# A two-block model on one core: reordering the activations, the gated scores and the output projection of the even mixer

## The chip, the core and the metric

The kernel runs on one core of a Trainium2 chip. The time is device time in microseconds (us) of that core, from one launch that computes the whole function. A profiled execution gives a span, which is the time between the first and the last thing the profiler records, and, beside it, the execution's own device time, which is a few us longer.

The engines named below are TensorE (PE in the profile; its weight loads are PEld), VectorE (DVE), ScalarE (ACT), GpSimd (POOL) and the queues that start DMAs. Each engine executes its own instructions in order and waits on semaphores that others raise.

## What is computed

The input is 256 tokens of width 1024. A first block (recurrent and attention halves) is followed by a second block of two layers. Layer 0 of the second block has the even mixer, which is what the change touches:

```python
def even_mixer(u, w_in, w_out, lb, onorm_g, sinks, cos_b, sin_b):
    B, S, _ = u.shape
    qa, fa, ia, ga, qb, kb, vb = jnp.split(u @ w_in, EVEN_SPLITS, axis=-1)
    oa = hgrn2_chunkwise(qa.reshape(B, S, A_HEADS, A_DK), fa.reshape(B, S, A_HEADS, A_DK),
                         ia.reshape(B, S, A_HEADS, A_DV), lb.reshape(A_HEADS, A_DK))
    oa = rmsnorm(oa, onorm_g) * jax.nn.silu(ga.reshape(B, S, A_HEADS, A_DV).astype(jnp.float32))
...
    ob = swa_with_sinks(qh, kh, vb.reshape(B, S, B_KV_HEADS, B_HEAD_DIM), sinks).astype(u.dtype)
    return jnp.concatenate([oa, ob], axis=-1) @ w_out
```

with 4 heads of 128 in the gated attention and 8 of 64 in the window attention. Inside the gated attention, for chunks of 64 tokens:

```python
    qf = jax.nn.silu(chunks(q))
    f = lb5 + (1.0 - lb5) * jax.nn.sigmoid(chunks(f_logit))
    k = 1.0 - f
...
    b = jnp.cumsum(jnp.log(f), axis=3)
    b_last = b[:, :, :, -1:, :]
    q_s = qf * jnp.exp(b)
    k_s = k * jnp.exp(-b)
    k_d = k * jnp.exp(b_last - b)
...
    att = jnp.where(causal, jnp.einsum('bhnck,bhnsk->bhncs', q_s, k_s), 0.0)
```

After the mixer come a residual add with a norm, and a feed-forward network (FFN) whose first step needs the normed rows of each token tile.

## The kernel before

Every engine's program is written out by hand in `build`, one block for each engine, and semaphores order them against each other. No scheduler moves anything.

**Weights as units.** All large weights are cut into units of 128 x 2048 floats (1 MB). SyncE loads them into a ring of 4 slots. For each unit ScalarE writes a rounded copy (`whi`, line 420, the helper `hi()`), then VectorE the rest (`wlo = raw - whi`, line 1190, the helper `lo()`), and TensorE multiplies in three passes (lines 2063 to 2065). `hi()` for unit u waits until TensorE has used unit u-4, `lo()` waits for `hi()`, and each engine takes the units in the order in which its program calls the helper. A helper that is called late holds back everything behind it on its engine.

**Token tiles.** The 256 tokens are two tiles of 128, t = 0 and t = 1. `acc[t]` are the PSUM sums. `turn` holds two PSUM buffers for transposes (line 2116), which are used in the order of the list `EVEN_TURNS`, and `aux` two for scores and mixes.

**The even mixer on TensorE.** Its program is a list of 34 slots, 0 to 33; a slot is one unit against one tile, 12 matmuls of 128 x 512 (slot 0 and 4 have some more). Slots 8 to 15 make the forget logits and queries (`fq`), 16 to 23 the values and output gates (`ig`), 24 and 25 a projection for the next layer (`ple1`, unit 12), 26 to 29 the output projection of the window attention (`out_swa`, units 13 and 14, both tiles), 30 to 33 that of the gated attention (`out_hgrn`, units 15 and 16). Small pieces are hooked in ahead of certain slots: the last two window mixes (`swa_mix`, line 2463) at 20 and 22, the last turns of probabilities at 19 and 21, `swa_fed` (transposes of the window output) at 25 and 27, `hgrn_scores` (line 2476, 4 heads) at 26, `hgrn_mix` (lines 2486 and 2489) at 27, `hgrn_fed` at 29 and 31, and `normed_rows` (eight transposes of tile 0 for the FFN) at 33.

**The even mixer on ScalarE.** After the exponentials of the last window head pair (`probs(3)`) stand: Silu of the queries `qsT` (line 905), Sigmoid of the forget logits `fT` (908), `probs_turned(2)` (two copies, 866, for which the mix at slot 20 waits), Ln (912), `values(0)` (844, 846), one `hi()` (unit 12), `probs_turned(3)`, three Exp of 128 x 1024 (`eb`, `ks`, `ebd`, 918 to 921), two `hi()` (units 13 and 14), and `values(1)`. A function of another table set than the last one costs an ACT_TABLE_LOAD ahead of it.

**The even mixer on VectorE.** `kk` from `fT`, `head_out(2)` (the output of window head pair 2), four scans that give b in `fT` (1902), `ebd` (1920), one `lo()` (unit 12), `head_out(3)`, then the scaled queries and keys: `qsT*eb` (1928), `ks` (1929), `kx`, `ky`, `kz` (1932 to 1940). The last of them raises `keys_ready`, for which `hgrn_scores` waits. Then two `lo()` and, per head, the masked copy of the scores `att_a` (1951).

**The tail.** When the last slot of tile 0 is done, ScalarE squares `acc[0]`, GpSimd forms the norm's scale, and VectorE scales, adds to `h` and writes the normed rows `xn` (1253, 1260, 1244), which `normed_rows` transposes.

Of the kernel before, what the change touches and what calls it, by code (L numbers as in the profile page):

```python
# [26 lines left out]
P = 128  # L27
# [87 lines left out]
def build(nc, io):  # L115
    with ExitStack() as ctx:
# [286 lines left out]
        def _(act):  # L403
# [404 lines left out]
            def even():  # L808
# [94 lines left out]
                for name in ("g0", "g1"):  # L903
                    received(name)
                act.activation(qsT[:, :, :], qsT[:, :, :], ACT.Silu).then_inc(q_silu, 1)
# [9 lines left out]
                hi()  # L915
                probs_turned(3)
                act.wait_ge(b_ready, 1)
                act.activation(eb[:, :, :], fT[:, :, :], ACT.Exp).then_inc(ea_ready, 1)
                act.activation(ks[:, :, :], fT[:, :, :], ACT.Exp, scale=-1.0).then_inc(ea_ready, 1)
                act.wait_ge(ebd_in, 1)  # L920
                act.activation(ebd[:, :, :], ebd[:, :, :], ACT.Exp).then_inc(ea_ready, 1)
                hi(2)
# [11 lines left out]
                hi()  # L934
                fed("s1", 4, 1)
                for t in range(TOK):
                    mix()
                    act.activation(xn[:, t, 0:BANK], aux[:, t, :], ACT.Square).then_inc(sq_ready, 1)
                fed("h0", 0, 0)
                hi(2)  # L940
# [3 lines left out]
                square_sum(acc[0][:, :], xn[:, 0, :])  # L944
                feed(feed_hi, 0)
# [223 lines left out]
        def _(dve):  # L1169
# [632 lines left out]
            def even():  # L1802
# [123 lines left out]
                dve.wait_ge(q_silu, 1)  # L1926
                dve.wait_ge(ea_ready, 2)
                mark(dve.tensor_tensor(qsT[:, :, :], qsT[:, :, :], eb[:, :, :], ALU.mult))
# [13 lines left out]
                lo(2)  # L1942
                no_sums(1)
                no_sums(0)
                fed("s0", 4, 0)
                lo()
                no_sums(1, 1)
                for a in range(A_HEADS):
                    n["aux"] += 1
                    dve.wait_ge(aux_ready, n["aux"])  # L1950
                    dve.copy_predicated(att_a[:, a, :], mask_a[:, :].bitcast(I32), aux[:, a % 2, 0:3 * P])\
                        .then_inc(aux_read, 1)
                lo()
                fed("s1", 4, 1)
# [5 lines left out]
                for t in range(TOK):  # L1960
                    dve.wait_ge(rstdm_ready, t + 1)
                    for a in range(A_HEADS):
                        ins = dve.scalar_tensor_tensor(ymix[:, t, P * a:P * a + P], aux[:, t, P * a:P * a + P],
                                                       rsm[:, t, a:a + 1], sga2[:, t, a, :], ALU.mult, ALU.mult)
                        if a < A_HEADS - 1:
                            mark(ins)
                        if a == A_HEADS - 2:
                            settle()
                    ins.then_inc(hgrn_out, 1)
                fed("h0", 0, 0)  # L1970
                lo(2)
# [6 lines left out]
                lo()  # L1978
# [74 lines left out]
        def _(pe):  # L2053
# [350 lines left out]
            def even():  # L2404
# [62 lines left out]
                def hgrn_scores():  # L2467
                    pe.wait_ge(keys_ready, 1)
                    pe.wait_ge(swa_p, B_HEADS // 2)
                    for a in range(A_HEADS):  # L2470
# [45 lines left out]
                slots += [("out_swa", 13 + k, k, t) for t in range(TOK) for k in range(2)]  # L2516
                slots += [("out_hgrn", 15 + k, k, t) for t in range(TOK) for k in range(2)]
                for s, (kind, k, i, t) in enumerate(slots):
# [18 lines left out]
                    if s in SWA_SCORES:  # L2537
                        swa_scores(SWA_SCORES.index(s))
                    if s == 25:
                        swa_fed(0)  # L2540
                    if s == 26:
                        hgrn_scores()
                    if s == 27:
                        swa_fed(1)
                        hgrn_mix()
                    if s in (29, 31):
                        hgrn_fed(0 if s == 29 else 1)
# [238 lines left out]
```

## Time and profile before

| | |
|---|---|
| median of 3 runs | 1446.43 us (1443.91 to 1447.07) |
| profiled execution, device time | 1445.71 us |
| its span | 1442.9 us |
| TensorE busy | 1414.0 us (98%), 6598 matmuls |
| VectorE busy | 871.1 us (60%) |
| ScalarE busy | 711.4 us (49%) |
| GpSimd busy | 79.7 us (6%) |
| DMA | 272.51 MB, mean 189 GB/s |

TensorE's matmuls overlap: a record is longer than the distance to the next start. So its busy share says that it hardly ever stands still, and the useful numbers are the starts in the timeline and the idle time in square brackets, with the engine that ended it. Times within the span count from its start. The even mixer fills the stretch from about 510 to 624 us.

### The profile page before, as it was taken

How to read it: one execution, taken by the hardware profiler on the slowest of the kernel's cores; microseconds unless marked ns; L12 is line 12 of the kernel's file. 1: busy time of each engine (PE TensorE's matmuls, PEld its weight loads, DVE VectorE, ACT ScalarE, POOL GpSimd, SP SyncE). 2: the span in 40 equal slices, each digit the busy share in tenths (PEclk: the TensorE clock that was granted, in tenths of full speed). 3: DMA queues.
4: the chain of work that ended last, by engine and by line, in shares of the span. 5: the costliest groups of instructions: out<-in, count | busy, mean ns of one | idle time of the engine just before them, and what ended most of it. 6: DMA issues, size and time to landing. Idle time of an engine off the chain costs nothing.

```text
span 1442.9 us, 17115 instructions
## 1 busy us (share of the span) xinstructions
PE 1414.0 (98%) x6598; PEld 1169.2 (81%) x6598; DVE 871.1 (60%) x811; ACT 711.4 (49%) x724; POOL 79.7 (6%) x91
## 2 busy tenths in 40 slices
PE   7999999999999999999999999999999999999997
PEld 6788887878888888878888878888888878888886
DVE  6869686776453766764644574644674545654536
ACT  4674765545343457653443553443543445453424
POOL 0000000010000200110000120000202101000001
PEclk9999999999999999999999999999999999999999
DMA  9747554465464553444555464555463533654541
GB/s 393 292 153 262 184 177 158 164 238 212 168 222 156 190 197 117 152 176 182 204 185 186 182 236 173 213 189 184 172 216 134 207 143 124 241 179 170 196 184 44
DMA packets 40380, 272.51 MB, mean 189 GB/s; under 512 B 4609, under 2 KB 5505, under 8 KB 8706
## 3 DMA queue, kind: packets, MB, share of 16 engines
q1 hardware_dynamic: 36864, 261.65, 49.7%
q10 hardware_dynamic: 3458, 10.04, 2.2%
q8 instruction: 42, 0.69, 0.2%
q14 instruction: 16, 0.13, 0.0%
HBM read 270.62 MB, written 1.05 MB: 188 GB/s over the span
## 4 chain that ended last, share of the span: by engine, by line
PE 85%; DVE 7%; ACT 3%; DMA 3%; issue 2%; POOL 0%; SPq 0%; DVEq 0%; POOLq 0%; ACTq 0%
PE acc L2063 26%; PE acc L2065 26%; PE acc L2064 26%; PE turn L2116 3%; DVE wlo L1190 3%; DMA raw<-in_units 2%; ACT whi L420 1%; DMA mod_raw<-in_units 1%; DVE h L1260 1%; DVE xn L1244 1%; PE aux L2600 0%; PE turn L2265 0%; DVE feed_lo L1228 0%; DMA gpost<-in_g_final 0%; DVE xn L1253 0%
## 5 line engine op out<-in xcount | busy, mean ns | idle before, releaser
L1190 DVE TENSOR_TENSOR wlo<-raw,whi 128x2048 fp32r<-128x2048 f32 x233 | 533.0, 2297 | 260.3 <-ACT whi L420 260.2
L2063 PE MATMUL acc<-whi,feed_hi 128*128 128x512 f32 (+1 forms) x1496 | 595.6, 398 | 4.9 <-DVE wlo L1190 4.4
L2065 PE MATMUL acc<-whi,feed_lo 128*128 128x512 f32 (+1 forms) x1496 | 583.1, 390 | 0.0
L2064 PE MATMUL acc<-wlo,feed_hi 128*128 128x512 f32 (+1 forms) x1496 | 582.2, 389 | 0.0
L420 ACT ACTIVATE whi<-raw 128x2048 fp32r<-128x2048 f32 x233 | 445.4, 1916 | 256.1 <-PE acc L2065 241.1
L2063 PEld LDWEIGHTS acc<-whi,feed_hi 128*128 128x128 f32 x1496 | 281.9, 188 | 65.7 <-DVE wlo L1190 6.8
L2065 PEld LDWEIGHTS acc<-whi,feed_lo 128*128 128x128 f32 x1496 | 281.5, 188 | 59.8
L2064 PEld LDWEIGHTS acc<-wlo,feed_hi 128*128 128x128 f32 x1496 | 282.2, 189 | 55.9 <-issue 1.2
L2063 PE MATMUL acc<-whi,hid_hi 128*128 128x512 f32 x352 | 138.0, 392 | 0.0
L2065 PE MATMUL acc<-whi,hid_lo 128*128 128x512 f32 x352 | 137.1, 389 | 0.0
L2064 PE MATMUL acc<-wlo,hid_hi 128*128 128x512 f32 x352 | 137.0, 389 | 0.0
L2065 PEld LDWEIGHTS acc<-whi,hid_lo 128*128 128x128 f32 x352 | 66.1, 188 | 13.8
L2064 PEld LDWEIGHTS acc<-wlo,hid_hi 128*128 128x128 f32 x352 | 66.1, 188 | 13.3
L2063 PEld LDWEIGHTS acc<-whi,hid_hi 128*128 128x128 f32 x352 | 66.1, 188 | 13.3
L679 ACT ACTIVATE hid_hi<-turn 128x512 f32 (+2 forms) x48 | 26.4, 549 | 99.3 <-PE turn L2116 99.3
L1704 DVE TENSOR_TENSOR hid_lo<-turn,hid_hi 128x512 f32 (+2 forms) x48 | 30.8, 642 | 71.8 <-ACT hid_hi L679 71.8
L1090 POOL TENSOR_SCALAR ms<-ss 128x1 f32<-128x1 f32 x18 | 13.6, 756 | 1045.5 <-ACT xn L440 1025.7
L1695 DVE SCALAR_TENSOR_TENSOR hid<-acc,pre_rs,sgl 128x512 f32<-128x512 f32 (+1 forms) x48 | 33.8, 704 | 48.6 <-ACT sgl L672 44.7
L462 ACT ACTIVATE feed_hi<-turn 128x512 fp32r<-128x512 f32 x48 | 26.1, 593 | 55.1 <-PE turn L2116 55.1
L1228 DVE TENSOR_TENSOR feed_lo<-turn,feed_hi 128x512 fp32r<-128x512 f32 x48 | 31.0, 686 | 30.9 <-ACT feed_hi L462 30.8
L672 ACT ACTIVATE sgl<-acc,pre_rs 128x512 f32<-128x512 f32 x40 | 27.2, 680 | 37.6 <-PE acc L2065 37.6
L2116 PE MATMUL turn<-setup,xn 128*128 128x128 f32 x250 | 34.9, 279 | 5.0 <-DVE xn L1244 4.2
(326 smaller groups left out, 860.2 us busy)
## 6 DMA issues: line engine op xcount, KB each, us to landing
raw<-in_units SPq DMA_DIRECT2D x237, 1024.0 KB, 4.9
mod_raw<-in_units SPq DMA_DIRECT2D x6, 1024.0 KB, 10.9
gpost<-in_norm_g ACTq DMA_DIRECT2D x8, 512.0 KB, 4.4
gpre<-in_norm_g ACTq DMA_DIRECT2D x6, 512.0 KB, 5.6
mod_more<-in_units SPq DMA_DIRECT2D x2, 1024.0 KB, 23.4
h<-in_x SPq DMA_DIRECT2D x2, 512.0 KB, 10.3
w_ax<-in_w_ax SPq DMA_DIRECT2D x1, 1024.0 KB, 26.4
bgate<-in_b_gate SPq DMA_DIRECT2D x1, 1024.0 KB, 27.7
```

What stands on the lines that cost most here:

```text
L420: act.activation(whi[:, u % RING, :], raw[:, u % RING, :], ACT.Copy).then_inc(hi_ready, 1)
L462: act.activation(dst[:, 4 * i:4 * i + 4, lanes(t)], turn[:, b, :].rearrange("p (c s) -> p c s", c=4), ACT.Copy).then_inc(fed_hi, 1)
L672: act.activation(sgl[:, t, :, :], acc[t][:, :].rearrange("p (i n) -> p i n", i=2)[:, :, 0:256], ACT.Silu, scale=pre_rs[:, t:t + 1]).then_i ...
L679: act.activation(dst, turn[:, b, 0:P * count].rearrange("p (c s) -> p c s", c=count), ACT.Copy).then_inc(fed_hi, 1)
L1190: dve.tensor_tensor(wlo[:, u % RING, :], raw[:, u % RING, :], whi[:, u % RING, :].bitcast(F32), ALU.subtract).then_inc(lo_ready, 1)
L1228: dve.tensor_tensor(dst[part], turn[:, b, :].rearrange("p (c s) -> p c s", c=4), hi_part[part].bitcast(F32), ALU.subtract).then_inc(moved[ ...
L1695: dve.scalar_tensor_tensor(hid[:, t, 0:tiles, :], up, pre_rs[:, t:t + 1], sgl[:, t, 0:tiles, :], ALU.mult, ALU.mult)\
L1704: dve.tensor_tensor(hid_lo[:, at, lanes(t)], turn[:, b, 0:P * count].rearrange("p (c s) -> p c s", c=count), hid_hi[:, at, lanes(t)].bitca ...
L2063: pe.matmul(out, xh, wh, start=first, stop=False)
L2064: pe.matmul(out, xh, wl, start=False, stop=False)
L2065: return pe.matmul(out, xl, wh, start=False, stop=last)
L2116: last = pe.transpose(turn[:, b, P * i:P * i + P], part, ident[:, :])
```

## The change

Four things are moved; no arithmetic is added or removed.

1. ScalarE: the Silu of the queries goes from ahead of the Sigmoid to behind the three Exps. The Exp of `ks` now comes before that of `eb`. The `hi()` of unit 12 goes from behind `values(0)` to behind the three Exps, ahead of the Silu.
2. VectorE: `qsT*eb` becomes the last step of the keys instead of the first. `keys_ready` is now raised twice, by `kz` and by `qsT*eb`, and the scores wait for the second.
3. TensorE: the scores of heads 0 and 1 are made at slot 24, those of heads 2 and 3 at slot 25 (all four at 26 before). `hgrn_mix` is at 26 (27 before), `hgrn_fed` at 28 and 30 (29 and 31 before). VectorE's masked copies and the `lo()`, `hi()` and feeding steps around them are put in an order that fits.
4. The eight slots of the output projection are interleaved. Slots 26 to 33 were: window tile 0 twice, window tile 1 twice, gated tile 0 twice, gated tile 1 twice. They are now: window tile 0 twice, window tile 1 (unit 13), gated tile 0 twice (units 15 and 16), window tile 1 (unit 14), gated tile 1 twice. Tile 0 is summed at the end of slot 30 instead of 31, so that two slots lie between its sum and `normed_rows` at slot 33 instead of one.

```diff
@@ ScalarE
                 probs(3)
-                for name in ("g0", "g1"):
-                    received(name)
-                act.activation(qsT[:, :, :], qsT[:, :, :], ACT.Silu).then_inc(q_silu, 1)
                 for name in ("f0", "f1"):
                     received(name)
                 act.activation(fT[:, :, :], fT[:, :, :], ACT.Sigmoid).then_inc(f_sig, 1)
...
                 values(0)
-                hi()
                 probs_turned(3)
                 act.wait_ge(b_ready, 1)
+                act.activation(ks[:, :, :], fT[:, :, :], ACT.Exp, scale=-1.0).then_inc(ea_ready, 1)
                 act.activation(eb[:, :, :], fT[:, :, :], ACT.Exp).then_inc(ea_ready, 1)
-                act.activation(ks[:, :, :], fT[:, :, :], ACT.Exp, scale=-1.0).then_inc(ea_ready, 1)
                 act.wait_ge(ebd_in, 1)
                 act.activation(ebd[:, :, :], ebd[:, :, :], ACT.Exp).then_inc(ea_ready, 1)
+                hi()
+                for name in ("g0", "g1"):
+                    received(name)
+                act.activation(qsT[:, :, :], qsT[:, :, :], ACT.Silu).then_inc(q_silu, 1)
                 hi(2)
                 values(1)
...
-                hi()
-                fed("s1", 4, 1)
                 for t in range(TOK):
                     mix()
                     act.activation(xn[:, t, 0:BANK], aux[:, t, :], ACT.Square).then_inc(sq_ready, 1)
+                hi()
+                fed("s1", 4, 1)
                 fed("h0", 0, 0)
-                hi(2)
+                hi()
                 fed("h1", 0, 1)
                 sums(0)
                 square_sum(acc[0][:, :], xn[:, 0, :])
+                hi()
                 feed(feed_hi, 0)
@@ VectorE
                 head_out(3)
-                dve.wait_ge(q_silu, 1)
-                dve.wait_ge(ea_ready, 2)
-                mark(dve.tensor_tensor(qsT[:, :, :], qsT[:, :, :], eb[:, :, :], ALU.mult))
+                dve.wait_ge(ea_ready, 1)
                 mark(dve.tensor_tensor(ks[:, :, :], kk[:, :, :], ks[:, :, :], ALU.mult))
...
                     .then_inc(keys_ready, 1)
-                lo(2)
+                dve.wait_ge(q_silu, 1)
+                dve.tensor_tensor(qsT[:, :, :], qsT[:, :, :], eb[:, :, :], ALU.mult).then_inc(keys_ready, 1)
+                lo()
...
+                attend((0, 1))
                 fed("s0", 4, 0)
+                attend((2, 3))
                 lo()
                 no_sums(1, 1)
-                for a in range(A_HEADS):
...
                 lo()
-                fed("s1", 4, 1)
...
+                fed("s1", 4, 1)
+                lo()
                 fed("h0", 0, 0)
-                lo(2)
+                lo()
                 fed("h1", 0, 1)
...
                 feed(feed_lo, feed_hi, 0)
-                lo()
+                lo(2)
@@ TensorE
-                def hgrn_scores():
-                    pe.wait_ge(keys_ready, 1)
+                def hgrn_scores(heads):
+                    pe.wait_ge(keys_ready, 2)
...
-                slots += [("out_swa", 13 + k, k, t) for t in range(TOK) for k in range(2)]
-                slots += [("out_hgrn", 15 + k, k, t) for t in range(TOK) for k in range(2)]
+                swa, hgrn = ([[(kind, at + k, k, t) for k in range(2)] for t in range(TOK)]
+                             for kind, at in (("out_swa", 13), ("out_hgrn", 15)))
+                slots += swa[0] + swa[1][0:1] + hgrn[0] + swa[1][1:2] + hgrn[1]
...
+                    if s == 24:
+                        hgrn_scores((0, 1))
                     if s == 25:
                         swa_fed(0)
+                        hgrn_scores((2, 3))
                     if s == 26:
-                        hgrn_scores()
+                        hgrn_mix()
                     if s == 27:
                         swa_fed(1)
-                        hgrn_mix()
-                    if s in (29, 31):
-                        hgrn_fed(0 if s == 29 else 1)
+                    if s in (28, 30):
+                        hgrn_fed(0 if s == 28 else 1)
```

How the rows stand on the engines. On ScalarE, from the second half of `values(0)` to the two `hi()` behind the exponentials, before:

```order
L846 ACTIVATE sga_143<-acc,pre_rs 128x512
L420 ACTIVATE whi<-raw 128x2048 [waits unit_used,loaded1]
L866 ACTIVATE pt_147<-turn 128x384 [waits turned0,swa_mixed]
L866 ACTIVATE pt_147<-turn 128x384 [waits turned1]
L918 ACT_TABLE_LOAD
L918 ACTIVATE eb<-fT 128x1024 [waits b_ready]
L919 ACTIVATE ks<-fT 128x1024
L921 ACTIVATE ebd<-ebd 128x1024 [waits ebd_in]
L420 ACTIVATE whi<-raw 128x2048 [waits unit_used,loaded2]
L420 ACTIVATE whi<-raw 128x2048 [waits unit_used,loaded3]
```

and now:

```order
L846 ACTIVATE sga_143<-acc,pre_rs 128x512
L866 ACTIVATE pt_147<-turn 128x384 [waits turned0,swa_mixed]
L866 ACTIVATE pt_147<-turn 128x384 [waits turned1]
L914 ACT_TABLE_LOAD
L914 ACTIVATE ks<-fT 128x1024 [waits b_ready]
L915 ACTIVATE eb<-fT 128x1024
L917 ACTIVATE ebd<-ebd 128x1024 [waits ebd_in]
L420 ACTIVATE whi<-raw 128x2048 [waits unit_used,loaded1]
L921 ACT_TABLE_LOAD
L921 ACTIVATE qsT<-qsT 128x1024 [waits moved1]
L420 ACTIVATE whi<-raw 128x2048 [waits unit_used,loaded2]
L420 ACTIVATE whi<-raw 128x2048 [waits unit_used,loaded3]
```

The rounding of unit 12 (`whi`, loaded1) has moved from ahead of the exponentials to behind them, and the Silu with a table load has come in behind it.

On VectorE, from `ebd` over the `lo()` of unit 12 and `head_out(3)` to the first key, now; the order of these is as before, save that `ks` has taken the place of `qsT*eb` in the last row:

```order
L1921 TENSOR_TENSOR ebd<-fT 128x1024 [waits b_ready]
L1191 TENSOR_TENSOR wlo<-raw,whi 128x2048 [waits hi_ready]
L1849 TENSOR_TENSOR den<-den,esink 128x2x2 [waits sink_exp,swa_p]
L1851 RECIPROCAL rden<-den 128x2x2 [waits dve_step]
L1857 TENSOR_TENSOR ymix<-turn,rden 128x2x64 [waits swa_mixed,dve_step]
L1857 TENSOR_TENSOR ymix<-turn,rden 128x2x64 [waits swa_mixed]
L1928 TENSOR_TENSOR ks<-kk,ks 128x1024 [waits ea_ready]
```

The `wlo` of unit 12 has not moved: it still stands ahead of all keys and waits for the `whi` above.

On TensorE, the beginning of slot 24, before:

```order
L2063 MATMUL acc<-whi,feed_hi 128x512
L2064 MATMUL acc<-wlo,feed_hi 128x512
L2065 MATMUL acc<-whi,feed_lo 128x512
L2063 MATMUL acc<-whi,pT_hi 128x512 [waits lo_ready,ple_lo,acc_free0]
L2064 MATMUL acc<-wlo,pT_hi 128x512
```

and now:

```order
L2070 MATMUL acc<-whi,feed_hi 128x512
L2071 MATMUL acc<-wlo,feed_hi 128x512
L2072 MATMUL acc<-whi,feed_lo 128x512
L2483 MATMUL aux<-qsT,ks 128x64 [waits swa_p,keys_ready,acc_free0]
L2483 MATMUL aux<-qsT,kx 128x64
```

The wait for the keys stood two slots and one set of four transposes later; it now stands ahead of slot 24.

## Rows read from the trace of the kernel before

**Rows 1.** Waits of TensorE, 560 to 640 us: waiting <- waited for: total, times, longest
```profile
PE turn L2116 <- DVE xn L1244: 2.1, 2, 1.4
PE turn L2463 <- ACT pt L866: 1.0, 1, 1.0
PE aux L2476 <- DVE att_a L1951: 0.3, 1, 0.3
```
**Rows 2.** TensorE timeline, slots 19 to 24: start, length, line, operation [idle before]
```profile
566.49 0.39 PE L2065 MATMUL acc<-whi,feed_lo 128*128 128x512 f32 x1
567.87 0.41 PE L2463 MATMUL turn<-vb,pt 128*128 128x64 f32 x2 [0.99 <-ACT pt L866]
...
572.06 0.82 PE L2116 MATMUL turn<-setup,s 128*128 128x128 f32 x6
...
582.31 0.39 PE L2063 MATMUL acc<-whi,pT_hi 128*128 128x512 f32 x1
```
**Rows 3.** TensorE timeline, slots 32 and 33 and the FFN's first units
```profile
616.87 0.39 PE L2064 MATMUL acc<-wlo,feed_hi 128*128 128x512 f32 x1
617.10 0.39 PE L2065 MATMUL acc<-whi,feed_lo 128*128 128x512 f32 x1
...
620.65 0.48 PE L2063 MATMUL acc<-whi,feed_hi 128*128 128x512 f32 x1
...
631.64 1.03 PE L2116 MATMUL turn<-setup,xn 128*128 128x128 f32 x8
632.99 0.50 PE L2063 MATMUL acc<-whi,feed_hi 128*128 128x512 f32 x1 [0.32 <-DVE wlo L1190]
```
**Rows 4.** ScalarE timeline, 562 to 583 us
```profile
562.62 1.28 ACT L905 ACT_TABLE_LOAD   x1
...
565.00 1.28 ACT L908 ACT_TABLE_LOAD   x1
...
567.26 0.85 ACT L866 ACTIVATE pt<-turn 128x384 f32<-128x384 f32 x2
...
572.55 1.90 ACT L420 ACTIVATE whi<-raw 128x2048 fp32r<-128x2048 f32 x1
...
575.21 1.28 ACT L918 ACT_TABLE_LOAD   x1
576.51 1.06 ACT L918 ACTIVATE eb<-fT 128x1024 f32<-128x1024 f32 x1
...
579.37 3.70 ACT L420 ACTIVATE whi<-raw 128x2048 fp32r<-128x2048 f32 x2
```
**Rows 5.** VectorE timeline, from the scans to the end of the keys
```profile
570.05 2.58 DVE L1902 TENSOR_TENSOR_SCAN fT<-reset_a,ff 128x256 f32<-128x256 f32 x4 [0.33 <-ACT ff L912]
...
574.48 2.29 DVE L1190 TENSOR_TENSOR wlo<-raw,whi 128x2048 fp32r<-128x2048 f32 x1 [0.58 <-ACT whi L420]
576.69 0.16 DVE L1848 TENSOR_TENSOR den<-den,esink 128x4 f32<-128x4 f32 x1
...
578.62 1.23 DVE L1928 TENSOR_TENSOR qsT<-qsT,eb 128x1024 f32<-128x1024 f32 x1 [1.03 <-ACT ks L919]
579.76 1.22 DVE L1929 TENSOR_TENSOR ks<-kk,ks 128x1024 f32<-128x1024 f32 x1
...
583.49 4.49 DVE L1190 TENSOR_TENSOR wlo<-raw,whi 128x2048 fp32r<-128x2048 f32 x2
```
**Rows 6.** Stretches: bounds, length, busy of PE, PEld, DVE, ACT, POOL, granted PEclk, DMA
```profile
1435.00:1436.00 1.00, 0.65 (x3) 0.19 (x1) 0.00 (x0) 0.32 (x1) 0.00 (x0) 1.00 0.00 0
1437.00:1438.00 1.00, 0.00 (x0) 0.00 (x0) 0.77 (x2) 0.72 (x2) 0.00 (x0) 0.94 0.00 0
1438.00:1439.00 1.00, 0.00 (x0) 0.00 (x0) 0.00 (x0) 0.00 (x0) 0.81 (x2) 0.50 0.00 0
17.00:18.00 1.00, 0.51 (x3) 0.51 (x3) 1.00 (x2) 0.56 (x2) 0.35 (x1) 1.00 0.99 410
```
**Rows 7.** TensorE timeline, the longest idle time between matmuls near the start
```profile
17.49 1.66 PE L2191 MATMUL aux<-ones,mod_part 128*128 128x1 f32 x7 [2.92 <-DVE mod_part L1312]
```

More of the change, by code:

```diff
@@ L1941, in even, with attend @@
                     .then_inc(keys_ready, 1)
-                lo(2)
+                dve.wait_ge(q_silu, 1)
+                dve.tensor_tensor(qsT[:, :, :], qsT[:, :, :], eb[:, :, :], ALU.mult).then_inc(keys_ready, 1)
+                lo()
+                def attend(heads):
+                    for a in heads:
+                        n["aux"] += 1
+                        dve.wait_ge(aux_ready, n["aux"])
+                        dve.copy_predicated(att_a[:, a, :], mask_a[:, :].bitcast(I32), aux[:, a % 2, 0:3 * P])\
+                            .then_inc(aux_read, 1)
                 no_sums(1)
                 no_sums(0)
+                attend((0, 1))
                 fed("s0", 4, 0)
+                attend((2, 3))
                 lo()
                 no_sums(1, 1)
-                for a in range(A_HEADS):
[L1949 to L1952, printed above, removed]
                 lo()
-                fed("s1", 4, 1)
                 for t in range(TOK):
@@ L2465, in swa_mix @@
                         pe.matmul(out[1], pt2[:, j, 2 * P:], vb[:, 1, kv], start=False, stop=True).then_inc(swa_mixed, 1)
-                def hgrn_scores():
-                    pe.wait_ge(keys_ready, 1)
+                def hgrn_scores(heads):
+                    pe.wait_ge(keys_ready, 2)
                     pe.wait_ge(swa_p, B_HEADS // 2)
-                    for a in range(A_HEADS):
+                    for a in heads:
                         n["aux"] += 1
```

## The prediction

> **What bounds the kernel now.** I read the table of engines first: TensorE is busy nearly all of the span and no other engine is near it, so only what makes TensorE wait, or adds work to it, can move the time. Then the waits of TensorE in the stretch that the change touches: 3.4 us in all, three entries [rows 1]. Then its timeline, to see where each lies, and last the timelines of ScalarE and VectorE there, since a step moved on them costs nothing until TensorE has to wait for it. A matmul record is 0.39 us long, but the next starts 0.23 us after it (616.87 to 617.10 [rows 3]); so a wait costs its recorded idle time plus 0.16 us, or plainly the distance of the starts less 0.23.
>
> **Part 1: the Silu leaves the place ahead of the Sigmoid.** The mix at slot 20 starts 1.38 us after the matmul ahead of it (566.49 to 567.87) where 0.23 is normal, because the two copies `pt` come late [rows 2]. Ahead of the copies stand the Silu and its table load, from 562.62 to 565.00, 2.38 us [rows 4]. Without them the copies run from 564.88 for 0.85 us to 565.73, and TensorE comes at 566.72: the wait goes whole, **-1.15 us**, with 1 us to spare. One table load (1.28 us) goes from ScalarE too, since the queries' Silu and the gates' Silu now follow each other with nothing but copies between; ScalarE is not what ends anything there, so I count nothing for it.
>
> **Part 2: the scores in two halves.** The third head's scores waited 0.3 us for VectorE's masked copy [rows 1]. Between the halves there are now twelve matmuls of slot 24, some 2.7 us, and the wait goes: **-0.46 us**. In exchange TensorE changes once more between small and large matmuls, under 0.1 us, which I leave out.
>
> **Part 3: the interleaved output.** From the last matmul of slot 32 to the first behind the eight transposes are 3.55 us (617.10 to 620.65 [rows 3]), in which both halves of the normed rows are waited for. Eight transposes without that wait take at most 1.03 us (631.64 to 632.99 less the 0.32 that is another wait [rows 3]). So the wait is 3.55 - 0.23 - 1.03 = 2.29 us. The change puts a slot of 2.7 us more between tile 0's sum and these transposes, which is more than the wait: **-2.29 us**. The feeds of the gated output come one slot earlier, but so does the mix, and VectorE's unit steps between are the same in number; I see nothing new that is late. VectorE now has two units instead of one between the tails of tile 0 and tile 1. That is 2.2 us later for tile 1 (one `wlo`, 574.48 to 576.69 [rows 5]), of which most falls into time in which TensorE still multiplies; the wait for the FFN's fourth unit, 0.32 us now [rows 3], grows by 0 to 1.1. I take **+0.2 us**.
>
> **Part 4: the keys must be there at slot 24.** This is the term that the change adds. Slot 24 starts at 582.31 [rows 2], and without part 1's wait at **581.16**. The keys hang on this chain, in the new order:
>
> - the turns at slot 21 start at 572.06 - 1.15 = 570.91 and take 0.82 [rows 2], the second `pt` copy ends some 0.43 later (half of the 0.85 for two [rows 4]): 572.2. The scans are no later: they begin behind `head_out(2)` at about 568.6 and take 2.58 [rows 5], 571.2.
> - table load up to the next ScalarE start, 1.30 (575.21 to 576.51), and three Exps, 2.86 (576.51 to 579.37) [rows 4]: 576.4.
> - the `hi()` of unit 12, which the change puts here, 1.90 [rows 4]: 578.3.
> - the `lo()` of unit 12, which stands on VectorE ahead of all keys and has not moved, so it waits for that `hi()`: 2.21 [rows 5], 580.5. The `hi()` stood at 572.55 before [rows 4], and this `lo()` at 574.48.
> - `head_out(3)`, 0.90 (576.69 to 578.62 less the 1.03 of waiting), then the keys `ks` to `kz`, 3.73 (579.76 to 583.49) [rows 5]: 585.1. ScalarE's Silu is done by then (578.3 + 1.28 + about 1.1 = 580.7), so it is hidden.
> - `qsT*eb`, 1.23 [rows 5]: **586.4**.
>
> TensorE therefore stands still ahead of slot 24 for 586.4 - 581.2 = **+5.2 us**. Behind the waiting matmul are queued slot 24 itself, the window feed and everything after. Before, the same wait lay at slot 26, about 6 us later, and was met with 4.7 us to spare (583.5 against 588.2, two slots and four transposes behind 582.31). The chain's steps are measured ones; what can shift is their places, by 1 us either way.
>
> A ScalarE table switch is priced at about 2.66 us in all, load and drain, by the Trainium skill, "ScalarE: Activation LUTs", section "What ACT_TABLE_LOAD costs". The trace does not agree: the next function starts 1.30 us after the load [rows 4], and the trace decides. By the page's figure the stall would be 6.6 us instead of 5.2.
>
> **The sum without the clock:** -1.15 - 0.46 - 2.29 + 0.2 + 5.2 = **+1.5 us**. Against the profiled execution (1445.71 us, 2.8 above its span) that is 1447.2; against the median of the runs shown, which is 0.7 higher, 1447.9.
>
> **The clock.** A stop of 5.2 us is longer than any between matmuls so far. At the end of the kernel the last matmul ends at 1435.65; the granted clock is 1.00 still in 1436, 0.94 in the stretch 1437 to 1438 and 0.50 after [rows 6]: it fell to the lower level (1.2 GHz of 2.4) 2.2 us after the work ended. Near the start an idle time of 2.92 us passed with the clock at 1.00 [rows 6, 7]. So a fall within 5.2 us is likelier than not. How long TensorE then works at the lower level before it is given 2.4 GHz again, no row shows. I bound it by nothing below and by the length of the stop above, 5.2 us; half of such time is lost, 0 to 2.6 us. I take the middle, **+1.3 us**, which gives +2.8 and **1449.2 us**.
>
> The Trainium skill states the same rule, "TensorE: Matmul & The Clock Gate", section "What's actually happening": the throttled state is the default and activity releases it. It speaks against a change that makes one long stop out of several short ones, also where their sums are equal.
>
> **Rivals.**
>
> - *The clock holds.* For it: it held through 2.92 us. Against it: 5.2 is far longer, and it fell after 2.2 at the end. Then +1.5: 1447.9 us, or down to 1446.9 if the chain is 1 us shorter than I read it.
> - *The clock stays low for long (slower).* The place is slots 24 to 26, behind the stop. From 2.8 us at the lower level on, the loss passes 2.9 us in all; at 5.2 us it is +4.1: 1450.5 us. The scores and slot 24 then take twice their time.
> - *The keys are early (faster).* If the `lo()` of unit 12 did not have to wait for the late `hi()`, VectorE would take it at about 572.4, behind `ebd`, and be through `head_out(3)` at 575.6; the keys would be done at 579.3, and `qsT*eb` would wait for the Silu, 580.7, and end at 581.9. The stop would be 0.8 us, with no fall of the clock, and the sum -1.15 - 0.46 - 2.29 + 0.2 + 0.8 = -2.9: 1443.5 us. Against it: the order of rows shows both helpers where they stand, and `lo()` reads what `hi()` writes. It would take a fault in the reading of units.
> - *The change doesn't do what it says:* the order shows every move as described; I give it nothing.
>
> **How the numbers follow.** What a measurement can tell from no change is about 0.2%, 2.9 us. Forecast (stop, and a clock low for up to 2.8 us): 0.40. Clock holds: 0.23. Clock low for longer: 0.25. Keys early: 0.12. The forecast lies at the edge of 2.9 us, so a part of it, 0.08, counts as slower. Faster 0.12, within 0.2% 0.55, slower 0.33. The range leaves out the keys that are early and the far end of the low clock: from 1445.5 (the clock holds, the chain 1 us shorter, and the runs' own spread of 1 to 2 us) to 1451.0.
>
> **What would show it.** In the profile of the changed kernel TensorE's largest wait is ahead of the first score matmul at slot 24, about 5 us, ended by VectorE's `qsT*eb`; the waits for `pt`, `att_a` and the normed rows are gone; on VectorE `wlo` of unit 12 waits for `whi` some 6 us after `ebd`; a few us at a granted clock of 0.50 stand around slot 24. I am wrong if that wait is under 3 us, if the normed rows are still waited for, or if a new wait stands at slots 26 to 32.

## The result, and the profile after

The changed kernel takes 1451.61 us (median of 6 runs, 1450.29 to 1452.90) against 1446.12 us for the kernel before (6 runs): a ratio of 1.004, with a 95% interval of 1.003 to 1.005. It is slower by 5.5 us. The forecast was 1449.2 with a range up to 1451.0; the time lies 0.6 us above the range. Its profiled execution took 1451.58 us with a span of 1449.7.

TensorE's waits in the stretch of the change, 560 to 645 us of the changed kernel (waiting <- waited for: total, times, longest). Of the three entries in [rows 1] none is left; in their place:

```profile
PE aux L2483 <- issue: 5.2, 1, 5.2
PE acc L2070 <- DVE wlo L1191: 0.8, 1, 0.8
```

The timeline of TensorE at the end of slot 19 and around slot 24. The first pair answers to [rows 2]:

```profile
566.39 0.39 PE L2072 MATMUL acc<-whi,feed_lo 128*128 128x512 f32 x1
566.62 0.33 PE L2470 MATMUL turn<-vb,pt 128*128 128x64 f32 x2
...
580.76 0.39 PE L2072 MATMUL acc<-whi,feed_lo 128*128 128x512 f32 x1
586.36 0.66 PE L2483 MATMUL aux<-qsT,ks 128*128 128x64 f32 x2 [5.21 <-issue]
586.81 0.63 PE L2483 MATMUL aux<-qsT,kx 128*128 128x64 f32 x2
...
591.47 0.77 PE L2070 MATMUL acc<-whi,pT_hi 128*128 128x512 f32 x1
592.04 0.63 PE L2071 MATMUL acc<-wlo,pT_hi 128*128 128x512 f32 x1
592.47 0.63 PE L2072 MATMUL acc<-whi,pT_lo 128*128 128x512 f32 x1
```

The mix now starts 0.23 us after the last matmul of slot 19. The stop stands where it was forecast, from 580.76 + 0.23 to 586.36, and behind it everything runs at almost half the pace: a pair of score matmuls starts every 0.43 us instead of 0.22, a large matmul 0.43 us after the last instead of 0.23. The profile puts the wait down to "issue"; VectorE's timeline names what ended it. It answers to [rows 5]:

```profile
570.92 1.22 DVE L1921 TENSOR_TENSOR ebd<-fT 128x1024 f32<-128x1024 f32 x1
578.29 2.29 DVE L1191 TENSOR_TENSOR wlo<-raw,whi 128x2048 fp32r<-128x2048 f32 x1 [6.15 <-ACT whi L420]
...
581.31 1.22 DVE L1928 TENSOR_TENSOR ks<-kk,ks 128x1024 f32<-128x1024 f32 x1
...
585.04 1.22 DVE L1942 TENSOR_TENSOR qsT<-qsT,eb 128x1024 f32<-128x1024 f32 x1
```

`qsT*eb` ends at 586.26 and the scores start 0.1 us later. VectorE had stood still for 6.15 us ahead of the `lo()` of unit 12, waiting for ScalarE's rounding.

The stretches with TensorE's granted clock (bounds, length, busy time of PE, PEld, DVE, ACT and POOL, PEclk, DMA share, GB/s):

```profile
584.00:585.00 1.00, 0.00 (x0) 0.00 (x0) 0.97 (x3) 1.00 (x3) 0.00 (x0) 0.98 0.85 360
585.00:586.00 1.00, 0.00 (x0) 0.00 (x0) 1.00 (x2) 1.00 (x2) 0.00 (x0) 0.50 0.01 0
595.00:596.00 1.00, 1.00 (x5) 0.79 (x4) 0.00 (x0) 0.00 (x0) 0.00 (x0) 0.90 0.00 0
```

The clock fell to 1.2 GHz just before 585, four us after TensorE had stopped, and came back to 2.4 GHz at about 595.2. It was low for 10.2 us, and for 8.8 of them TensorE was at work. The other runs had it too: the mean granted clock was 0.992 to 0.994 in the six runs of the changed kernel, and 0.995 to 0.999 in 27 runs of the kernel before.

What part 3 gave is to be seen at the transposes of the normed rows: eight in one row, with no idle time ahead, where [rows 1] had two waits, 2.1 us in all. The second row is the wait that is left, for the FFN's fourth unit (0.77 us, against 0.32 in [rows 3]):

```profile
625.10 1.03 PE L2123 MATMUL turn<-setup,xn 128*128 128x128 f32 x8
...
638.67 0.50 PE L2070 MATMUL acc<-whi,feed_hi 128*128 128x512 f32 x1 [0.77 <-DVE wlo L1191]
```

That matmul starts at 638.67 against 632.99 before, 5.68 us later. The spans of the two profiled executions differ by more, 6.8 us, because a later stretch (842 to 860 us) had the clock low for 6.8 us in the one and 3.4 in the other; the table of stops below has this for every profile.

### The profile page after: what moved, and what is told of

Read it like the earlier page. It is cut to its first block, busy times and chain, and to the rows that moved or that the text cites. A ratio compares the mean times of both kernels' runs of the same rounds, so it can differ in the third digit from the quotient of the medians.

```text
span 1449.7 us, 17113 instructions
## 1 busy us (share of the span) xinstructions
PE 1418.2 (98%) x6598; PEld 1173.7 (81%) x6598; DVE 871.7 (60%) x811; ACT 710.3 (49%) x723; POOL 77.3 (5%) x91
## 4 chain that ended last, share of the span: by engine, by line
PE 89%; DVE 5%; DMA 3%; ACT 1%; issue 1%; POOL 1%; SPq 0%; DVEq 0%; POOLq 0%; ACTq 0%
PE acc L2070 27%; PE acc L2072 27%; PE acc L2071 27%; PE turn L2123 3%; DVE wlo L1191 2%; DMA raw<-in_units 2%; DMA mod_raw<-in_units 1%; PE aux L2483 1%; ACT whi L420 1%; PE aux L2610 0%; DVE h L1261 0%; DVE feed_lo L1229 0%; DVE xn L1245 0%; PE turn L2272 0%; DMA gpost<-in_g_final 0%
## 5 line engine op out<-in xcount | busy, mean ns | idle before, releaser
L1254 DVE SCALAR_TENSOR_TENSOR xn<-acc,gpost 128x1024 f32<-128x1024 f32 x12 | 14.7, 1223 | 40.3 <-ACT xn L440 40.3
```

## The experiments

The theory after the result (A): three short waits went as forecast; one stop of 5.4 us came, because the rounding of unit 12 was moved behind the exponentials on ScalarE while its other half still stands ahead of the keys on VectorE; the stop brought the clock down, and the low clock cost another 4 us. The rivals: the keys are too late for slot 24 in any order (B), and the slow matmuls behind the stop have another cause than the clock (C). Each run is compared with the kernel before on the same chip. The changed kernel was measured in a series of its own, so a difference of medians from it is good to some 0.4 us: the kernel before had a median of 1446.12 us there and 1445.71 in the first four runs below.

**Unit 12's rounding put back.** One line:

```diff
                 values(0)
+                hi()
                 probs_turned(3)
...
                 act.activation(ebd[:, :, :], ebd[:, :, :], ACT.Exp).then_inc(ea_ready, 1)
-                hi()
```

> The changed kernel with one helper put back: ScalarE rounds unit 12 behind values(0) again, ahead of the exponentials. Theory A (the stop at slot 24 is the chain through unit 12's rounding, its lo() and the keys): the lo() ends at about 573.6 instead of 580.5, head_out(3) then waits for the mix at slot 22 and ends at about 576, ks to kz end at 579.8, qsT*eb at 581.0, and TensorE arrives at 581.0: the stop shrinks from 5.2 to 0 to 0.5 us and the clock stays at its upper level around slot 24, so the kernel is 5.2 + 4.1 = 9 us faster than the changed one and 3 to 4 us faster than the one before (ratio 0.997 to 0.998). Rival B (the scores at slot 24 are too early whatever ScalarE's order, since the keys' own chain decides): a stop of over 3 us stays, and the kernel is within 2 us of the changed one (ratio 1.002 to 1.004).

Measured: 1442.82 us (11 runs), ratio 0.9983 (0.9974 to 0.9992): by the medians 2.9 us faster than before (2.5 by the ratio) and 8.8 us faster than the changed kernel. In the profiled execution the stop shrank from 5.2 to 0.74 us, and the granted clock stayed at 1.00 up to 1430 us:

```profile
582.01 0.41 PE L2483 MATMUL aux<-qsT,ks 128*128 128x64 f32 x2 [0.74 <-issue]
```

B falls. One misplaced step of 1.9 us on ScalarE made the whole loss. The 0.74 us that is left is more than the 0 to 0.5 expected: on VectorE the keys now waited 0.68 us for the third Exp, which I had left out.

**TensorE kept busy in the stop.** The keys come when they came; TensorE does work whose result is overwritten:

```diff
                     if s == 24:
+                        pe.wait_ge(swa_p, B_HEADS // 2)
+                        for _ in range(24):
+                            pe.matmul(aux[:, 0, 0:3 * P], ident_r[:, :], bias_r[:, :], start=True, stop=True)
                         hgrn_scores((0, 1))
```

> The changed kernel with 24 matmuls more on TensorE (128 x 384, into a score buffer that the scores overwrite) ahead of the wait at slot 24, so that TensorE works through most of the stop. The keys come when they came. Theory A (4.1 us of the loss is the clock, which falls in the stop and stays at 1.2 GHz until about 595 us): granted clock 1.00 from 580 to 600, the stop still ends at 586.4, and the kernel is 3 to 4.5 us faster than the changed one, about 1 us slower than the one before (ratio 1.000 to 1.002). Rival C (the matmuls behind the stop are slow for another reason, such as VectorE's and ScalarE's traffic, and the clock is incidental): scores at 0.43 us a pair as in the changed kernel, ratio 1.003 to 1.005.

Measured: 1447.56 us (11 runs), ratio 1.0017 (1.0008 to 1.0026). The medians are 4.05 us apart from the changed kernel's; each taken against its own kernel before, 3.6 us, and by the ratios 3.3. TensorE's timeline and its clock:

```profile
581.52 4.33 PE L2550 MATMUL aux<-bias_r,ident_r 128*128 128x384 f32 x24
586.84 0.43 PE L2483 MATMUL aux<-qsT,ks 128*128 128x64 f32 x2 [0.99 <-DVE qsT L1942]
587.11 0.39 PE L2483 MATMUL aux<-qsT,kx 128*128 128x64 f32 x2
```
```profile
584.00:586.00 2.00, 1.85 (x11) 1.53 (x9) 1.93 (x6) 2.00 (x4) 0.00 (x0) 1.00 0.70 295
586.00:590.00 4.00, 3.16 (x26) 3.12 (x27) 3.72 (x4) 1.72 (x1) 0.00 (x0) 1.00 0.00 0
```

The stop ended as late as in the changed kernel (586.84 here, 586.36 there), the scores then ran at 0.22 us a pair, and the clock held. So C falls, and the loss is split in two. Without the fall of the clock the kernel is 1.85 us slower than the one before by the medians (2.5 by the ratio); this is what the prediction called the sum without the clock, +1.5. The fall costs the rest, 3.3 to 4.05 us. The two traces price it more closely: from the first score matmul to the FFN's fourth unit TensorE takes 48.20 us here (586.84 to 635.04) and 52.31 in the changed kernel (586.36 to 638.67), 4.1 us more.

**The other end of the chain cut.** ScalarE as in the changed kernel, VectorE's `lo()` of unit 12 moved behind the keys:

```diff
-                lo()
                 head_out(3)
...
                 dve.tensor_tensor(qsT[:, :, :], qsT[:, :, :], eb[:, :, :], ALU.mult).then_inc(keys_ready, 1)
-                lo()
+                lo(2)
```

> The changed kernel with the other end of the same chain cut: ScalarE rounds unit 12 late as in the change, but VectorE takes its lo() behind qsT*eb instead of ahead of head_out(3). Theory A: head_out(3) ends at about 576, the keys at 579.8, qsT*eb waits for the Silu (580.6) and ends at 581.9, so the scores start after a stop of 0.9 us; two lo() then end at 586.4, but slot 24 itself needs the first of them, at 584.1, about when the scores of two heads end (584.5). Clock at its upper level. 7 to 9 us faster than the changed kernel, 2 to 3.5 us faster than before, ratio 0.9975 to 0.9985. Rival B (keys too early in any order): a stop of over 3 us stays.

Measured: 1442.73 us (10 runs), ratio 0.9986 (0.9977 to 0.9995), with a stop of 0.85 us, as worked out (0.9). The ratio is a hair above the expected 0.9975 to 0.9985; by the medians, 3.0 us, the gain is as expected. It is the same repair from the other side.

**Both ends late.** On top of that, the Silu ahead of unit 12's rounding:

```diff
-                hi()
                 for name in ("g0", "g1"):
                     received(name)
                 act.activation(qsT[:, :, :], qsT[:, :, :], ACT.Silu).then_inc(q_silu, 1)
-                hi(2)
+                hi(3)
```

> The changed kernel with unit 12 taken last on both engines: ScalarE makes the Silu right behind the exponentials and then rounds units 12 to 14; VectorE takes the lo() of unit 12 behind qsT*eb. Theory A (the chain through slot 21's turns, table load, three Exps and the keys is all that is left): exponentials end at 576.4, ks to kz at 579.9, the Silu at 578.8, qsT*eb at 581.1, TensorE arrives at 581.0: stop under 0.3 us against 0.7 and 0.85 in the two earlier repairs; the lo() of unit 12 ends at 583.3, before the scores of two heads end at 583.8. 0.5 to 1 us faster than those two, ratio to before 0.997 to 0.9985. Rival: the lo() of unit 12 is now late for slot 24 and a wait of over 0.5 us stands there; no gain on them.

Measured: 1442.51 us (11 runs), ratio 0.9981 (0.9972 to 0.9990). TensorE has no wait left from 560 to 600 us:

```profile
580.88 0.39 PE L2070 MATMUL acc<-whi,feed_lo 128*128 128x512 f32 x1
581.11 0.33 PE L2481 MATMUL aux<-qsT,ks 128*128 128x64 f32 x2
```

The stop is gone as expected. The trace shows what that is worth at this place: the FFN's fourth unit starts at 629.25, against 630.18 and 630.26 in the two repairs above, 0.9 to 1.0 us earlier. Whether the whole kernel is faster for it the times can't tell: the three intervals overlap almost wholly, and the expected gain of 0.5 to 1 us is smaller than they are. All three beat the kernel before and the changed one.

**The Silu's move alone**, on the kernel before: the Silu behind the exponentials, `ks` first, `qsT*eb` last, all else as it was. In short:

```diff
-                act.activation(qsT[:, :, :], qsT[:, :, :], ACT.Silu).then_inc(q_silu, 1)
...
                 act.activation(ebd[:, :, :], ebd[:, :, :], ACT.Exp).then_inc(ea_ready, 1)
+                act.activation(qsT[:, :, :], qsT[:, :, :], ACT.Silu).then_inc(q_silu, 1)
```

> Part 1 alone, on the kernel before: the Silu behind the exponentials, ks ahead of eb, qsT*eb last; unit 12, the scores at slot 26 and the order of the output slots as before. Theory A: the wait of 0.99 us for pt goes (TensorE 1.15 us earlier from slot 20 on), the scores at slot 26 find the keys in time, the waits for att_a (0.3) and for the normed rows (2.1) stay: 1.0 to 1.2 us faster than before, ratio 0.999. Rival: the keys now end later than slot 26 and a new wait of over 0.5 us appears there, ratio 1.000 or above.

This missed by far: 1451.22 us (4 runs), ratio 1.0041 (1.0025 to 1.0056), as slow as the changed kernel. The wait for `pt` went, but TensorE's waits from 560 to 640 us are now:

```profile
PE turn L2116 <- DVE xn L1244: 2.4, 2, 1.7
PE aux L2476 <- DVE att_a L1951: 1.8, 1, 1.8
PE turn L2116 <- ACT sga L846: 1.2, 1, 1.2
```

Two are new in size. The last is `values(1)`, which stands behind the Silu on ScalarE and frees `acc[1]` for slot 25. The second is VectorE's masked copy, late behind a `lo()` that began 0.86 us later than before (589.36 instead of 588.50, behind ScalarE's later feed) and also took 1.1 us longer. GpSimd's product of the gates with the norm's gain had begun just ahead of it: the gates' Silu no longer needs a table load, so GpSimd began at its old time (589.32 instead of 589.50) although the steps around it on ScalarE were 1.2 us late. VectorE and GpSimd in that run:

```profile
589.36 3.38 DVE L1190 TENSOR_TENSOR wlo<-raw,whi 128x2048 fp32r<-128x2048 f32 x1
```
```profile
589.32 4.55 POOL L1141 TENSOR_TENSOR sga<-sga,onorm_a 128x512 f32<-128x512 f32 x2 [81.04 <-ACT sga L931]
```

In the kernel before VectorE was there first, by 1.00 us, and GpSimd alone paid:

```profile
588.50 2.28 DVE L1190 TENSOR_TENSOR wlo<-raw,whi 128x2048 fp32r<-128x2048 f32 x1
```
```profile
589.50 3.65 POOL L1141 TENSOR_TENSOR sga<-sga,onorm_a 128x512 f32<-128x512 f32 x2 [81.51 <-ACT sga L931]
```

In the changed kernel the two products took 2.52 us (from 598.48), beside masked copies and the beginning of two `lo()`. Behind the waits of the Silu-only run the clock fell too (0.50 from 595 to 601 us, and again at 626). TensorE worked at the lower level for 9.9 us in all, which at nearly half a us each (0.43 against 0.23 us a matmul) is an estimated 4.6 us, most of this run's loss.

**GpSimd held back**, to test that reading. The run above with one wait more:

```diff
+                    pool.wait_ge(aux_read, A_HEADS)
                     for t in range(TOK):
                         pool.wait_ge(silu_ready, t + 1)
```

> The run with the Silu move alone, and GpSimd's product of the gates with the norm's gain held back until the four masked score copies are done. Theory D (in the Silu-only run the lo() of 3.38 us, the late att_a and TensorE's wait of 1.8 us come from GpSimd and VectorE working on the same memory at once): the lo() takes 2.3 us, TensorE's wait for att_a falls from 1.8 to about 0.7 us, and the clock keeps its upper level at 590 to 600 us or is low for less. Rival E (the att_a wait comes from ScalarE's late feed of the window output alone): the lo() may be short or long, the wait stays above 1.5 us.

Measured (one run): 1448.91 us. TensorE's row for the third head's scores, and VectorE's `lo()`:

```profile
591.89 0.43 PE L2477 MATMUL aux<-qsT,ks 128*128 128x64 f32 x2 [0.68 <-DVE att_a L1952]
```
```profile
589.06 2.28 DVE L1191 TENSOR_TENSOR wlo<-raw,whi 128x2048 fp32r<-128x2048 f32 x1
```

The wait fell from 1.77 to 0.68 and the `lo()` from 3.38 to 2.28 us, both as theory D of the expectation had it; the 0.38 us by which 0.68 is above the 0.30 of the kernel before belong to the later feed. The clock was still low for 6.8 us between 592 and 599, so the part of the expectation on the clock missed: the waits that remain (1.25 and 0.68 us within 7 us) were followed by it as well. In the changed kernel and its repairs TensorE has neither of the two waits, though VectorE and GpSimd still meet there: two `lo()` in a row take 5.55 us (from 599.80) instead of the 4.49 in [rows 5]. Which of the other edits hides the two costs was not tested. By the order of the rows it is the scores in two halves: the third head's masked copy then stands behind a slot instead of behind a `lo()`, and `values(1)` has the time of the scores.

**Without the interleaving.** The first repair with the output slots in the order of before:

```diff
-                swa, hgrn = ([[(kind, at + k, k, t) for k in range(2)] for t in range(TOK)]
-                             for kind, at in (("out_swa", 13), ("out_hgrn", 15)))
-                slots += swa[0] + swa[1][0:1] + hgrn[0] + swa[1][1:2] + hgrn[1]
+                slots += [("out_swa", 13 + k, k, t) for t in range(TOK) for k in range(2)]
+                slots += [("out_hgrn", 15 + k, k, t) for t in range(TOK) for k in range(2)]
```

> The repaired kernel (unit 12 rounded early) with the output slots in the order of before: window tile 0 twice, window tile 1 twice, gated tile 0 twice, gated tile 1 twice; scores, mix and feeds as in the change. Theory A (the interleaving is what hides the normed rows): the wait ahead of the transposes at slot 33 is back, 1.4 + 0.7 us of recorded idle time, 2.3 us slower than the repaired kernel, ratio to before 0.999 to 1.0005, plus 1.7 to 3.4 us if the clock falls there. Rival: the earlier gated output alone hides it, no wait, ratio as the repaired kernel.

Measured: 1445.77 us (10 runs), ratio 1.0003 (0.9994 to 1.0012), against 0.9983 (0.9974 to 0.9992) with the interleaving: about 2.9 us. The waits are back to the hundredth:

```profile
618.33 0.66 PE L2123 MATMUL turn<-setup,xn 128*128 128x128 f32 x4 [1.36 <-DVE xn L1245]
619.72 0.66 PE L2123 MATMUL turn<-setup,xn 128*128 128x128 f32 x4 [0.73 <-DVE xn L1245]
```

and the clock was low for 3.4 us behind them in the profiled execution; in that of the kernel before, the same two waits left it at 1.00. So the gain of part 3 is shown, 2.3 us of waits, and what the clock adds to it differs from one profile to the next.

**Stops of other lengths.** The first repair with `kz` computed one, three or five times more on VectorE, which delays `qsT*eb` (the cut shows the run with three). One profiled run each:

```diff
+                for _ in range(3):
+                    mark(dve.tensor_tensor(kz[:, :, :], ky[:, :, :], last_of(2).to_broadcast([P, A_HEADS, P]),
+                                           ALU.mult))
+                    settle()
```

> As the run with a stop of 2.9 us, with kz computed once more: a stop of 1.5 us ahead of slot 24. Theory A: the clock holds, span 0.7 us above the repaired kernel's; if it falls after so short a stop, waits of the kernel before (three within 5 us at 842) are the pattern.

> The repaired kernel with kz computed three times more on VectorE ahead of qsT*eb, each 0.73 us, so that the stop of TensorE ahead of slot 24 is 0.7 + 2.2 = 2.9 us. A stop as long as the one near the start of the kernel, in which the clock held. Theory A (a stop over some 2.2 us may bring the clock down, and it then stays down for more us than the stop lasted): either nothing, span 2.2 us above the repaired kernel's, or a low stretch of 3 to 9 us with 1.6 to 4.2 us lost on top. Rival F (only stops as long as 5 us do that): clock 1.00 throughout.

> As before, with kz computed five times more: a stop of 4.4 us. Theory A: the clock falls in the stop or just behind it and is low for 3 to 9 us while TensorE works, 1.6 to 4.2 us lost on top of the stop; the sum is then 5.2 to 8 us above the repaired kernel. Rival F (only stops as long as 5 us bring it down): clock 1.00, span 3.7 us above the repaired kernel's.

**The changed kernel once more:**

> The changed kernel once more, for another profile of the same program: theory A expects the stop of 5.2 us at the same place to within 0.1 us, and the low stretch behind it to differ, since the chip's clock does not follow the program's time: between 3 and 9 us with TensorE at work. Rival: it is 8.8 us again to within 0.3 us.

Measured: 1443.54, 1445.95 and 1451.93 us for the stops of 1.5, 2.9 and 4.4 us, and 1452.04 us for the changed kernel, one run each. The profiled executions, with the time at the lower level added up from stretches of half a us. The fourth column is the start of the FFN's fourth unit, behind slot 24 and ahead of the stretch at 842:

| kernel | stop at slot 24 | clock low around it | FFN's fourth unit | clock low at 842 to 860 | span |
|---|---|---|---|---|---|
| before | none (waits of 0.99 and 0.30) | 0 | 632.99 | 3.4 | 1442.9 |
| both ends late | 0 | 0 | 629.25 | 6.8 | 1440.8 |
| unit 12 put back | 0.74 | 0 | 630.18 | 0 | 1438.7 |
| stop 1.5 | 1.47 | 0 | 630.88 | 3.4 | 1441.6 |
| stop 2.9 | 2.92 | 6.8 | 635.40 | 0 | 1444.0 |
| stop 4.4 | 4.38 | 10.2 | 638.47 | 6.8 | 1450.1 |
| changed | 5.21 | 10.2 | 638.67 | 6.8 | 1449.7 |
| changed, again | 5.21 | 10.2 | 639.30 | 6.8 | 1450.2 |

The stops of 2.92, 4.38 and 5.21 us were each followed by a clock that was low for longer than the stop, those of 0.74 and 1.47 us were not. That is theory A, and rival F, by which only stops as long as 5 us do this, falls. Each case has one profile, the changed kernel two. At the FFN's fourth unit the stop of 1.5 us costs 0.70 us over the first repair, as expected (0.7), and that of 2.9 us 5.2 us, 2.2 for the stop and 3.0 for the clock, as expected too. The stop of 4.4 us costs 8.3 us there, 0.3 above the 5.2 to 8 expected: TensorE worked at the low level for 9.8 us. In the spans the differences are larger, 11.4 us for the stop of 4.4, mostly because the stretch at 850 was low as well, which it was not in the profile of the first repair. The changed kernel's two profiles gave the same 10.2 us, so in that run the rival of A was nearer: the clock came back at 596.0 instead of 595.2, and TensorE, which started at 586.76, worked at the low level for 9.3 us instead of 8.8.

The stop of 2.9 us shows one thing more. TensorE's row and its clock:

```profile
584.02 0.41 PE L2487 MATMUL aux<-qsT,ks 128*128 128x64 f32 x2 [2.92 <-issue]
```
```profile
584.00:585.00 1.00, 0.98 (x8) 1.00 (x9) 1.00 (x1) 1.00 (x3) 0.00 (x0) 0.91 0.00 0
585.00:586.00 1.00, 1.00 (x7) 1.00 (x7) 1.00 (x1) 1.00 (x2) 0.00 (x0) 0.50 0.00 0
591.00:592.00 1.00, 1.00 (x4) 0.76 (x4) 0.00 (x0) 0.00 (x0) 0.00 (x0) 0.68 0.00 0
```

The clock fell at about 584.8, when TensorE had been at work again for 0.8 us, and stayed low for 6.8 us of full work.

## Why the prediction failed, step by step

**What it had right.** The mechanism and the place of the terms: TensorE's only large wait is ahead of the first scores at slot 24, ended by `qsT*eb`; the chain runs through the late `hi()` of unit 12 and the `lo()` that did not move; the clock falls. The chain was forecast to end at 586.4 and ended at 586.26; of its inner marks the exponentials were forecast to end at 576.4, the `hi()` at 578.3, the `lo()` at 580.5 and the keys at 585.1, and the next steps began at 576.36, 578.29, 580.50 and 585.04.

**The terms.** Measured at the start of the FFN's fourth unit, where the changed kernel is 5.68 us later:

| term | forecast | measured |
|---|---|---|
| Silu, wait for `pt` | -1.15 | -1.15 (1.38 to 0.23 between the starts) |
| masked copy of the third head | -0.46 | -0.46 (no wait left) |
| normed rows | -2.29 | -2.29 (no wait left) |
| FFN's fourth unit | +0.2 | +0.45 (0.32 to 0.77) |
| stop at slot 24 | +5.2 | +5.37 (580.76 to 586.36, less 0.23) |
| clock | +1.3 | +4.2 |

Without the last line the sum is +1.9 instead of +1.5, and the run with a busy TensorE measured +1.85. The clock's 4.2 is from the rows: twelve score pairs took 586.36 to 591.47 = 5.11 us instead of 2.67 (at 0.22 a pair), and up to 595.2 some nine large matmuls started 0.43 apart instead of 0.23, 1.7 us. The comparison with the busy TensorE gave 4.1. The terms add up to 6.1 against the 5.68 measured. Of the 0.4 us between them 0.2 lie ahead of the stop, where TensorE was 1.33 us earlier than before (580.76 against 582.09) and not 1.15; the rest is not assigned.

**The step that failed** is the term of the clock: "How long TensorE then works at the lower level before it is given 2.4 GHz again, no row shows. I bound it by nothing below and by the length of the stop above, 5.2 us; half of such time is lost, 0 to 2.6 us." The term was mis-sized, +1.3 where it is 4.2, and its bound had no ground: TensorE worked at the lower level for 8.8 us, 1.7 times the stop. It was also wrong that no row shows it. The trace of the kernel before has such a stretch, behind three waits of 0.51, 0.73 and 1.55 us between 842 and 847, which the profile's page does not show, since it prints the clock in tenths for slices of 36 us. TensorE's timeline of the kernel before there, and its clock:

```profile
846.73 0.50 PE L2063 MATMUL acc<-whi,feed_hi 128*128 128x512 f32 x1 [1.55 <-DVE wlo L1190]
...
848.07 0.63 PE L2064 MATMUL acc<-wlo,feed_hi 128*128 128x512 f32 x1
848.50 0.63 PE L2065 MATMUL acc<-whi,feed_lo 128*128 128x512 f32 x1
```
```profile
848.00:849.00 1.00, 1.00 (x4) 0.74 (x3) 0.00 (x0) 0.00 (x0) 0.00 (x0) 0.50 0.80 115
850.00:851.00 1.00, 1.00 (x4) 0.76 (x4) 0.00 (x0) 0.00 (x0) 0.00 (x0) 0.61 1.06 414
```

A matmul starts 0.43 us after the last there, and the clock is low for 3.4 us while TensorE is always at work. Taken as a bound, that row would have put the lower end of the term at 1.6 us instead of 0, behind far shorter waits than 5.2 us, and the forecast on the slower side: +1.5 and at least 1.6 are over the 2.9 us. It also gives the price of a us at the low level: 1 - 0.23/0.43, nearly half, as I had it. And it speaks against the prediction's sentence that one long stop is worse than several short ones as a rule on the clock: three short waits were followed by a fall as well. What the long stops had more of here is the length of the low stretch, 6.8 and 10.2 us against 3.4.

**The rivals.** The one that came is "the clock stays low for long", which had a chance of 0.25. Its price, +4.1, still stopped at 5.2 us of low clock. In the same way the range's upper end, 1451.0, left out the far end of a bound that was itself too near. The rival "keys early" was not what the change does, but it is what it could have been: it was worked out at 1443.5, and the run that made it come true by the other end of the chain gave 1442.73, with a stop of 0.85 us where 0.8 was worked out.

**The table load.** One went from ScalarE, and I counted nothing for it. In the changed kernel that holds. In the Silu-only run the gates' Silu without its load let GpSimd begin just ahead of VectorE's `lo()`, and cost 1.1 us of TensorE's time (1.77 against 0.68 with GpSimd held back). The claim "ScalarE is not what ends anything there" looked only at what ScalarE itself ends, not at what its shorter queue lets another engine begin.

## What to carry to other kernels

When a step is moved on one engine, find its other half on the next engine's queue: a rounding that is put off by 6 us puts off everything that stands behind its consumer, also what has nothing to do with it. A stop of the engine that bounds the kernel is to be priced with what its clock does afterwards, and for that one looks up every stretch of the trace where the mean granted clock is below 1, however little, before the sum is made. Where the stop can't be avoided, work without use in it was worth about 4 us here; and a step that becomes earlier against its neighbours needs the same look as one that becomes later.

## What the runs showed of the hardware

- TensorE's clock fell behind waits that are short one by one: 0.51, 0.73 and 1.55 us within 5 us (the kernel before), 1.25 and 0.68 us within 7 us (GpSimd held back). It did not fall behind a single 0.74 or 1.47, nor, near the start, behind 2.92 us [rows 7]; behind 2.92 us at slot 24 it did, 0.8 us after TensorE was at work again. Behind waits of 1.36 and 0.73 us at the normed rows it held in the profile of the kernel before and fell in that of the run without the interleaving. So no length of one wait separates the cases in these runs. In 13 profiles (of twelve kernels) the stretch at 842 to 860, with nearly the same three waits, was low for 0 (twice), 3.4 (six times) or 6.8 us (five times).
- The low stretches that began in or behind short waits, and the one behind the stop of 2.92 us, lasted 3.4 or 6.8 us. Those that began within a stop lasted 10.2 us, the rest of the stop among them (changed kernel and stop of 4.4 us). TensorE was fully busy for up to 9.8 us (stop of 4.4 us) before it was given 2.4 GHz again.
- The Trainium skill, "TensorE: Matmul & The Clock Gate", section "What's actually happening", says that the throttled state is the default and that activity releases it. The runs agree: the low stretches within the kernels ended while TensorE was fully busy, after 8.8 us of work in the changed kernel, and the one behind the last matmul of the kernel before, from 1437.9 us on, did not end in the profile.
- VectorE and GpSimd slowed each other down when a `lo()` and GpSimd's products, both on tiles in SBUF, ran side by side. GpSimd first by 0.04 us (the Silu-only run): the `lo()` took 3.38 us instead of 2.28, the two products 4.55 instead of 2.52. VectorE first by 1.00 us (the kernel before): the `lo()` took 2.28 us, the products 3.65.
